# Second block's experts: twelve places for the weights' units, the result scaled on ScalarE, the next tokens turned earlier

## The reference

```python
def expert_choice_ffn(xn, w_router, w_gate, w_up, w_down):
    B, S, D = xn.shape
    cap = EC_CAPACITY * S // N_EXPERTS_2
    aff = jax.nn.softmax((xn @ w_router).astype(jnp.float32), axis=-1)
    g, idx = lax.top_k(aff.swapaxes(1, 2), cap)
    bidx = jnp.arange(B)[:, None, None]
    xs = xn[bidx, idx]
    hid = jax.nn.silu(jnp.einsum('becd,edf->becf', xs, w_gate)) * jnp.einsum('becd,edf->becf', xs, w_up)
    y = jnp.einsum('becf,efd->becd', hid, w_down) * g[..., None].astype(xn.dtype)
    return jnp.zeros_like(xn).at[bidx, idx].add(y)
```

## Time and profile before

| | |
|---|---|
| median of 3 runs | 3684.78 us (3678.25 to 3687.08) |
| the profiled execution's own time | 3693.22 us |
| its span in the profile | 3691.4 us |
| TensorE busy | 3382.4 us (92%) |
| VectorE busy | 2611.9 us (71%) |
| ScalarE busy | 2070.1 us (56%) |
| GpSimd busy | 375.1 us (10%) |
| low parts of the units, VectorE | 576.7 and 290.1 us, 384 instructions |
| high parts of the units, ScalarE | 477.1 and 246.4 us, 384 instructions |

### The profile page before, as it was taken

How to read it: one execution, slowest core, us unless ns; L and a number is a source line. 1 busy time by engine, 2 the same in 40 slices (tenths; PEclk the granted TensorE clock), 3 DMA queues, 4 the chain that set the end, 5 groups by cost and what they waited for, 6 DMA issues and landing times. The chain is left out here.

```text
span 3691.4 us, 53966 instructions
## 1 busy us (share of the span) xinstructions
PE 3382.4 (92%) x18672; PEld 2569.4 (70%) x18672; DVE 2611.9 (71%) x4216; ACT 2070.1 (56%) x3323; POOL 375.1 (10%) x300
## 2 busy tenths in 40 slices
PE   9999989699869998998699999899989996999996
PEld 5444667577758764876588888787648775788884
DVE  3997755788662366663899999722766638899996
ACT  2663551588631475552577777523755524777775
POOL 0012000122121002000011111010020000111110
PEclk9999899799989999999899999999999997999998
DMA  3000012776251101014699999611010136999997
GB/s 147 23 1 4 1 67 72 309 261 262 105 218 41 46 16 38 1 58 157 232 394 379 381 394 380 246 41 47 2 52 2 54 134 234 387 374 394 381 381 285
DMA packets 118370, 646.00 MB, mean 175 GB/s; under 512 B 17456, under 2 KB 20144, under 8 KB 65968
## 3 DMA queue, kind: packets, MB, share of 16 engines
q1 hardware_dynamic: 97744, 569.19, 39.4%
q0 software_dynamic: 15984, 58.20, 5.4%
q10 hardware_dynamic: 4464, 16.25, 1.1%
HBM read 581.21 MB, written 62.39 MB: 174 GB/s over the span
## 5 line engine op out<-in xcount | busy, mean ns | idle before, releaser
L3441 DVE TENSOR_TENSOR low_ring<-mix,high_ring 128x2048 fp32r<-128x2048 f32 x256 | 576.7, 2284 | 42.1 <-ACT high_ring L3390 42.1
L3390 ACT ACTIVATE high_ring<-mix 128x2048 fp32r<-128x2048 f32 x256 | 477.1, 1932 | 80.3 <-PEq L141 80.3
L3329 PE MATMUL ps<-high_ring,x_high 128*128 128x512 f32 x1024 | 408.6, 399 | 8.1 <-DVE low_ring L3441 5.0
L3331 PE MATMUL ps<-high_ring,x_low 128*128 128x512 f32 x1024 | 399.7, 390 | 0.0
L3330 PE MATMUL ps<-low_ring,x_high 128*128 128x512 f32 x1024 | 399.3, 390 | 0.0
L3441 DVE TENSOR_TENSOR low_ring<-more_raw,high_ring 128x2048 fp32r<-128x2048 f32 x128 | 290.1, 2285 | 24.5 <-ACT high_ring L3390 24.5
L3390 ACT ACTIVATE high_ring<-more_raw 128x2048 fp32r<-128x2048 f32 x128 | 246.4, 1925 | 0.0
L3329 PEld LDWEIGHTS ps<-high_ring,x_high 128*128 128x128 f32 x1024 | 192.2, 188 | 70.2 <-DVE low_ring L3441 17.5
L3331 PEld LDWEIGHTS ps<-high_ring,x_low 128*128 128x128 f32 x1024 | 192.2, 188 | 41.4
L3330 PEld LDWEIGHTS ps<-low_ring,x_high 128*128 128x128 f32 x1024 | 192.4, 188 | 37.6
L3329 PE MATMUL ps<-high_ring,h_high 128*128 128x512 f32 x512 | 205.9, 402 | 0.0
(11 more groups left out here) (514 smaller groups left out, 8061.0 us busy)
## 6 DMA issues: line engine op xcount, KB each, us to landing
mix<-in_expert_units SPq DMA_DIRECT2D x256, 1024.0 KB, 7.8
more_raw<-in_expert_units SPq DMA_DIRECT2D x128, 1024.0 KB, 8.6
raw_experts<-in_expert_units SPq DMA_DIRECT2D x16, 3072.0 KB, 11.3
expert_out<-out ACTq DMA_DIRECT2D x31, 512.0 KB, 2.7
qk_body<-residual SPq DMA_DIRECT2D x16, 512.0 KB, 7.6
mix<-in_w_turned SPq DMA_DIRECT2D x16, 512.0 KB, 3.6
qk_tail<-in_w_out SPq DMA_DIRECT2D x8, 1024.0 KB, 7.9
mix<-residual SPq DMA_DIRECT2D x16, 512.0 KB, 3.3
```

Of the source, the lines that this page charges most:

```text
L3329: nc.tensor.matmul(ps[:, bank, :], left_high, high, start=first, stop=False)
L3331: return nc.tensor.matmul(ps[:, bank, :], left_low, high, start=False, stop=final)
L3390: nc.scalar.activation(w_high[:, n % RING, :], raw[n % RAW_UNITS], ACT.Copy).then_inc(high_ready, 1)
L3441: nc.vector.tensor_tensor(w_low[:, n % RING, :], raw[n % RAW_UNITS], w_high[:, n % RING, :].bitcast(F32), ALU.subtract).then_inc(low_ready, 1)
```

## The change

Three things. First, there are twelve raw places, one for each unit, in a memory of their own (three tiles `raw_ring`), and the low part of a unit is written over its raw unit (`w_low` is the same memory, seen as rounded numbers). The load of a unit then has to wait until TensorE has used that unit of the expert before (`unit_used`), and all twelve units of expert 0 are loaded during `choose_tokens`. `taken`, `silu` and `hid` now lie in three rows of `mix` (`spare`), so the views will call all three `mix`. The ring of high parts keeps its six places. Second, the result is scaled on ScalarE, behind the split of unit 2 of the next expert; VectorE keeps only the copy of the gate's value, now behind unit 8. Third, TensorE turns the next expert's tokens right behind the second half of `hid`, before unit 9 and not after it.

```diff
-UNITS, UP_UNITS, RAW_UNITS = 12, 8, 6
+UNITS, UP_UNITS = 12, 8
...
         w_high = sb("high_ring", [P, RING, 2048], F32R)
-        w_low = sb("low_ring", [P, RING, 2048], F32R)
-        taken = sb("taken", [P, D])
+        taken, silu, hid = (spare[:, n, :] for n in range(3))
...
                 def load_unit(e, n):
 
-                    sp.wait_ge(low_ready, e * UNITS + n - RAW_UNITS + 1)
-                    sp.dma_start(raw[n % RAW_UNITS], expert_unit(A, layer, e, n)).then_inc(unit_in[n % RAW_UNITS], 16)
-
-
-                for n in range(RAW_UNITS, UNITS):
-                    load_unit(0, n)
+                    sp.wait_ge(unit_used, e * UNITS + n - UNITS + 1)
+                    sp.dma_start(raw[n], expert_unit(A, layer, e, n)).then_inc(unit_in[n], 16)
+
...
                     down_unit(e, 8)
                     turn_hid(e, 1)
-                    down_unit(e, 9)
                     if more:
                         turn_x(e + 1)
+                    down_unit(e, 9)
...
+                def finish(e, later):
+                    act.wait_ge(gate_ready, e + 1)
+                    act.wait_ge(unit_used, e * UNITS + UNITS)
+
+                    if later:
+                        act.wait_ge(summed, base + 16 * e)
+                    for h in range(2):
+                        nc.scalar.activation(out[:, tile(h, HALF)], ps[:, 6 + h, :], ACT.Copy,
+                                             scale=gcol[:, :]).then_inc(out_ready, 1)
...
                         if n == 12:
                             high_x(e + 1)
+                        if n == 14:
+                            finish(e, later)
+                    if not more:
+                        finish(e, later)
...
-                    nc.vector.tensor_tensor(w_low[:, n % RING, :], raw[n % RAW_UNITS],
+                    nc.vector.tensor_tensor(w_low[n % UNITS], raw[n % UNITS],
                                             w_high[:, n % RING, :].bitcast(F32), ALU.subtract).then_inc(low_ready, 1)
...
-                        if n == 13:
-                            finish(e, later)
-                    if not more:
-                        finish(e, later)
+                        if n == 8:
+                            gate_of(e, later)
...
+            with ExitStack() as same_place:
+                thirds = [sb(same_place, f"low_ring{n}", [P, 4, 2048], F32R) for n in range(3)]
+                w_low = [thirds[n // 4][:, n % 4, :] for n in range(UNITS)]
+            thirds = [sb(part, f"raw_ring{n}", [P, 4, 2048]) for n in range(3)]
+            raw = [thirds[n // 4][:, n % 4, :] for n in range(UNITS)]
```

More of the change, by code:

```diff
@@ L3215, in _, with unit_rows, experts_two @@
             nc.vector.tensor_tensor(index[:, :], apart[:, :], col(1, 0), ALU.add)
-UNITS, UP_UNITS, RAW_UNITS = 12, 8, 6
+UNITS, UP_UNITS = 12, 8
 def expert_unit(A, layer, e, n):
     return A["expert_units_2"][bass.ds((layer * EXPERTS + e) * UNITS + n, 1)].rearrange("a p f -> p (a f)")
-def unit_rows(ring, n):
-    return ring[:, n % ring.shape[1], :].rearrange("p (k f) -> p k f", k=4 if n < UP_UNITS else 2)
-def experts_two(book, ps, A, layer, taken_in, summed, kept, ident, gain, gates, index, raw, rows_dram, sum_dram):
+def unit_rows(unit, n):
+    return unit.rearrange("p (k f) -> p k f", k=4 if n < UP_UNITS else 2)
+def experts_two(book, ps, A, layer, taken_in, summed, kept, ident, gain, gates, index, raw, w_low, spare, rows_dram,
+                sum_dram):
     nc = book.nc
@@ L3254, in experts_two @@
         base = 16 * EXPERTS * layer
-        unit_sems = [f"unit{n}_in" for n in range(RAW_UNITS)]
+        unit_sems = [f"unit{n}_in" for n in range(UNITS)]
         with Stage(book, *unit_sems, "high_ready", "low_ready", "unit_used", "x_turned", "x_high_ready",
@@ L3326, in product @@
                 def product(bank, left_high, left_low, n, k, cols, first, final):
-                    high, low = unit_rows(w_high, n)[:, k, cols], unit_rows(w_low, n)[:, k, cols]
+                    high, low = unit_rows(w_high[:, n % RING, :], n)[:, k, cols], unit_rows(w_low[n], n)[:, k, cols]
                     nc.tensor.matmul(ps[:, bank, :], left_high, high, start=first, stop=False)
@@ L3382, in split @@
                 def split(e, n, later):
[L3385 to L3386 removed]
+                    if later or n >= UNITS:
+                        act.wait_ge(unit_in[n % UNITS], 16 * e + 16 * (n // UNITS))
                     if later or n >= RING:
                         act.wait_ge(unit_used, e * UNITS + n - RING + 1)
[L3390 removed]
+                    nc.scalar.activation(w_high[:, n % RING, :], raw[n % UNITS], ACT.Copy).then_inc(high_ready, 1)
                 def high_x(e):
@@ L3467, in low_hid, with gate_of @@
                                             ALU.subtract).then_inc(h_low_ready, 1)
-                def finish(e, later):
+                def gate_of(e, later):
                     if later:
@@ L3473, in finish @@
                     nc.vector.tensor_copy(gcol[:, :], gates[:, bass.ds(e, 1)]).then_inc(gate_ready, 1)
[L3474 to L3481, removed]
                 def expert(e, later, more):
@@ L3707, in layer_two @@
         with ExitStack() as part:
-            more = sb(part, "more_raw", [P, RAW_UNITS - 4, 2048])
-            as_units = mix[:, :, :].rearrange("p (n a) d -> p n (a d)", a=2)
-            raw = [as_units[:, n, :] for n in range(4)] + [more[:, n, :] for n in range(RAW_UNITS - 4)]
+            with ExitStack() as same_place:
[3 more added lines that the diff above has]
+            raw = [thirds[n // 4][:, n % 4, :] for n in range(UNITS)]
             choose_tokens(book, ps, ident, logit[:, :, :], gates, index,
-                          [(expert_unit(A, layer, 0, n), raw[n]) for n in range(RAW_UNITS)])
-            experts_two(book, ps, A, layer, taken_in, summed, kept, ident, gain_f, gates, index, raw, A["normed"],
-                        A["residual"])
+                          [(expert_unit(A, layer, 0, n), raw[n]) for n in range(UNITS)])
+            experts_two(book, ps, A, layer, taken_in, summed, kept, ident, gain_f, gates, index, raw, w_low,
+                        mix, A["normed"], A["residual"])
 def finish_two(book, A, summed, stats, sb):
```

8 lines of the change are left out of this document (3 added, 5 removed).

## The result

The changed kernel takes 3789.66 us (median of four, 3784.41 to 3800.23) against 3684.16 (median of four, 3678.25 to 3687.08): a ratio of 1.0295 [1.0278, 1.0312], 105 us slower. The forecast was 3678.5 in a range of 3666 to 3696.

The account below looks back on a forecast made before the run. TensorE, busy 456.94 of 459.76 us, with DMA at 0.99, was taken as bound. Of 12.9 us the gather left 4.2, plus 1.8 (tipping point) and 0.13 per layer: 6.3, so 3678.5 from the median; range 3666 to 3696.

Parts of the forecast that it names:

- The stall at unit 2: TensorE's wait for unit 2's low part at experts 1 to 15, both layers: goes, 0.43 us each, 12.9 us.
- The scaling on ScalarE: Behind next unit 2's split: starts S + 0.63, takes 1.28 us, hidden in ScalarE's 1.43 us idle time, costs nothing.
- S: Start of an expert's first product on TensorE, from which the prediction counts its times.
- The chain behind it: GpSimd's scatter landing, index copy, gather: gather lands S + 26.13, 0.65 us late for the turning; 35.23 us per expert.
- the prediction's own tipping point: Index copy ahead of unit 7's split: gather lands S + 25.2, expert takes 34.94; one expert in five, 1.8 us.
- Twelve places: Loads into twelve raw places, low parts in place, twelve loads under the choice of tokens: nothing gained or lost.
- The early turning: Next tokens turned one unit sooner on TensorE: waits for the gather, gives gain back; 0.14 us left per expert, 4.2.
- Slower: Rival, chance 0.15: the gather lands late at the turning; 3711 at a 10.0 us gather, 3732 at 10.7.
- The rule cited: VectorE instruction with two SBUF inputs blocks GpSimd's SBUF reads; if it did not hold, the full 12.9 us.
- Full gain: Rival, chance 0.27: gather lands 0.65 us sooner or index copy slips ahead of split; 34.94 per expert, 13 us, 3671.5.

Follow-up runs that it names:

- e5: The changed kernel plus one wait: VectorE waits for its own low part of unit 2 before unit 3's split; 3667.94 us, 0.9966 of the kernel before.
- e10: The changed kernel plus one VectorE wait for its own last split, ahead of unit 4's split; 3673.79 us, 0.9968 of the kernel before.
- e11: The changed kernel plus one VectorE wait for its own last split, ahead of unit 2's split; 3672.10 us, 0.9971 of the kernel before.
- e4: The kernel before with only the scaling moved to ScalarE and the gate's copy behind unit 8; six places, late turning; 3787.65 us, 1.0291.
- e3: The kernel before with only the twelve places and low parts written in place; 3683.53 us, 1.000.
- e7: The kernel before with only the next tokens turned ahead of unit 9; 3693.39 us, 1.0027.
- e2: The changed kernel with the scaling back on VectorE ahead of next unit 2's split; 3687.15 us, 1.0012 of the kernel before.
- e8: The changed kernel with a VectorE wait ahead of unit 3's split and the turning back behind unit 9; 3669.69 us, 0.9957 of the kernel before.
- e9: The kernel before with scaling on ScalarE, gate's copy behind unit 8 and a VectorE wait ahead of unit 3's split; 3664.73 us, 0.9945.
- e12: The changed kernel with a VectorE wait ahead of unit 3's split and tokens' high and low parts made one unit sooner; 3667.55 us, 0.9963.

## Why the prediction was wrong

It was wrong by one step, the length of the scatter's issue.

- **The stall at unit 2.** Right. The rows for `low_ring` at 0.7 us are gone and the undisturbed experts take 34.87 us where 34.94 was worked out.
- **The scaling on ScalarE.** Right. Counted from S = 1906.70 it starts at S + 0.56 (0.63 worked out), takes 1.31 us (1.28) and the scatter's issue starts at S + 2.68 (2.71), under a split of unit 2 that runs from S + 1.98 to S + 4.27.
- **"At 1936.92 VectorE runs the first of two splits, to 1938.32; the issue takes 2.86 and ends 1.46 behind that. After, the split of unit 2 runs from S + 1.98 to S + 4.26, so the issue ends at S + 5.72 instead of S + 7.33."** This is the step that failed. It ends at S + 12.34. I took the end of the split in flight as the point that lets the issue go, since all the rows I had were of a split behind a break. It was not the first of two splits either, but of four: behind the two of the earlier trace rows the timeline of the kernel before goes on without a gap.

```profile
1940.44 4.48 DVE L3441 TENSOR_TENSOR low_ring<-more_raw,high_ring 128x2048 fp32r<-128x2048 f32 x2
```

So before the change too three more splits ran on behind the one in flight, and the issue did get through, as the first split's. The change takes the break ahead of unit 2 away: the gate's copy and the scaling on VectorE had stood between unit 1's split and unit 2's. With them gone the split of unit 2 is the second of five, and the issue is held to the end of the fifth. e5, e10 and e11 place the gap and move the end of the issue with it; e4 has this part alone and the whole loss. Whether the copy of 0.15 us alone would have been break enough, left where it was, no run tests.
- **The chain behind it.** The order was right and each link moved as worked out from the wrong start: landing, index copy at S + 21.28 (14.37), gather at S + 22.66 (17.13), turning at S + 32.56. Two terms of it were off besides. The gather's issue took 2.34 us in the one expert and 2.29 in the next, both under a split, where the sum had 1.00, and it landed after 9.9 us in the median and not 9.0. In e5, where only the held issue is mended, the scatter in turn lands in 9.7 us (median) and not 11.1: the gather starts at 1942.23, S + 14.89, lands near S + 24.8, and TensorE turns at 1952.88, S + 25.54, without a wait. That is the prediction's own tipping point: the index copy goes ahead of unit 7's split and the gather's issue hangs on that split, over near S + 17.2. It had been given one expert in five; in e5 it holds for 11 of the first layer's 14 gathers.
- **Twelve places.** Right, worth nothing (e3). The lists in `choose_tokens` still take 35.89 us.
- **The early turning.** Right that it gives the gain back while the gather is late: e7 costs 11 us and e2, with the same scaling, is 5 us slower than the kernel before. With the run broken it is worth nothing either way (e5 against e8).
- **The rivals.** *Slower* named the right wait, TensorE at the tokens' turning, but priced it by the spread of a gather, 3696 to 3732. Most of the delay wasn't the gather's own: it landed 0.9 us slower, but its issue started 5.5 us late, because of the scatter ahead of it. Nothing in that rival looked at what else on VectorE could hold GpSimd. The text does say that the sum fails if those waits pull the clock down, and this happened: 1.90 of the 8.9 us per long expert.
- **The rule cited.** The page "SBUF — State Buffer" of the Trainium skill, section "Who interferes with whom", has a VectorE instruction with two SBUF inputs block a GpSimd instruction that reads SBUF. I read it as one instruction blocking. The runs show the issue held over a whole run of them, 9.66 us, unless it starts under the first.

The size of *Full gain* (13 us, 3671.5) is what e5, e8, e9 and e11 then gave, 10 to 20 us (3664.7 to 3672.1), but only with one wait added.

## What to carry to other kernels

Moving work off an engine also takes away the break that this work made in the engine's stream. Before moving it, list what GpSimd issues there: here its issue of a scatter lived on the break that 1.41 us of scaling (and the gate's copy) made, and the way to keep both is a wait of VectorE for its own last instruction, 0.12 us. The pace alternated between two values here because the late gather, by the stall it caused, undid its own cause for one expert. Where a pace alternates, read the two kinds of period side by side: the difference stands there row by row.

## What the runs showed of the hardware

- Issues of one scatter on GpSimd took 1.59 us with no split running on VectorE. Started under a split (128x2048, two inputs in SBUF) they took 2.85 to 3.27 when it was the first of four, some 3.03 under the second of two (e5, e8, e9) or the third of three (e12), 4.89 to 5.27 under the second of three (e10), 9.33 to 9.68 under the second of five. In each the end lay 1.46 to 1.50 us behind the end of a split: of that first one, or of the last of the run. The first of the run stood behind VectorE's scaling, with no idle time between (before, e2, e3, e7), or behind a gap (e11). A gap of 0.12 us was enough. Why the first of a run lets go and a later one doesn't, no run shows.
- The gathers' issues follow the same rule at another distance: 1.00 us with no split running, and under a split an end 0.87 to 0.89 us behind that split or the last of its run. Five gathers started under the first of two and were let go at its end, as the one at 3179.26 in the earlier trace rows.
- In the changed kernel's stalls at the tokens' turning TensorE's granted clock fell to 0.50 while it waited and stood there for 6.8 us in twelve of the fourteen, for 10.2 us in the two longest (waits of 8.5 and 9.0 us).
- One core drew 386 to 390 GB/s over 460 us with its DMA engines at a share of 1.00 (e5, e8, e9, e11), a little over the 0.99 of the earlier trace rows; at 34.87 us per expert TensorE and the DMA engines are full together.
